# Rotary embedding of the attention queries and keys: half-turn by a permutation matmul, or by VectorE products that cross the partition halves

## The reference

```python
def _apply_rope(x, cos, sin):
    half = x.shape[-1] // 2
    x1, x2 = xf[..., :half], xf[..., half:]
    return jnp.concatenate([x1 * c - x2 * s, x2 * c + x1 * s], axis=-1)
...
def _dsa_branch(q, k, v, qi, ki, wi, rope_att, rope_idx, n_visible):
    q = _apply_rope(q.reshape(B_, T_, ATT_HEADS, ATT_HD), cos_a, sin_a)
    k = _apply_rope(k.reshape(B_, T_, ATT_KV_HEADS, ATT_HD), cos_a, sin_a)
    qi = _apply_rope(qi.reshape(B_, T_, IDX_HEADS, IDX_HD), cos_i, sin_i)
    ki = _apply_rope(ki.reshape(B_, T_, 1, IDX_HD), cos_i, sin_i)[:, :, 0]
    ...
        s = jnp.einsum('bqhd,bsd->bqhs', qib, ki)
        s = jnp.einsum('bqhs,bqh->bqs', jax.nn.relu(s), wib)
        _, idx = lax.top_k(s, topk)
        logits = jnp.einsum('bqgrd,bqkgd->bqgrk', qg, k_sel) * (ATT_HD ** -0.5)
        p = jax.nn.softmax(jnp.where(valid, logits, -jnp.inf), axis=-1)
        o = jnp.einsum('bqgrk,bqkgd->bqgrd', p, v_sel)
```

## Time and profile before

| what | us |
|---|---|
| time, median of 3 runs (lowest to highest) | 1267.67 (1267.56 to 1268.07) |
| profiled execution, first to last instruction | 1268.2 |
| TensorE busy in it | 1254.3 |
| VectorE busy | 919.6 |
| ScalarE busy | 699.2 |
| GpSimd busy | 154.3 |

### The profile page before, as it was taken

The page is one execution under the profiler, slowest core; times in us unless marked ns, Lnnn a source line. Parts: engine busy times, 40 slices in busy tenths (PEclk is TensorE's granted clock), DMA queues, the critical chain, the costliest instruction groups (busy, mean ns, idle before and its releaser), DMA issues.

```text
span 1268.2 us, 23324 instructions
## 1 busy us (share of the span) xinstructions
PE 1254.3 (99%) x9041; PEld 1169.6 (92%) x9041; DVE 919.6 (73%) x1290; ACT 699.2 (55%) x1082; POOL 154.3 (12%) x113
## 2 busy tenths in 40 slices
PE   9999999999999999999999999999999999999998
PEld 8997999999989998889998989999889998999986
DVE  6886874878778774447734547999758777999954
ACT  5556465654456343345354546666547567766642
POOL 0000142000000000000000001642200000464310
PEclk9999999999999999999999999999999999999999
DMA  7552332322355555555553444555564444454562
GB/s 300 189 173 101 133 134 101 133 68 68 152 197 188 195 179 185 198 170 182 183 209 109 156 173 167 198 169 195 194 221 171 162 154 163 167 188 175 197 224 93
DMA packets 30315, 212.83 MB, mean 168 GB/s; under 512 B 3488, under 2 KB 3616, under 8 KB 5152
## 3 DMA queue, kind: packets, MB, share of 16 engines
q1 hardware_dynamic: 29088, 206.53, 46.9%
q0 software_dynamic: 1152, 5.24, 1.1%
HBM read 210.71 MB, written 1.05 MB: 167 GB/s over the span
## 4 chain that ended last, share of the span: by engine, by line
PE 86%; DVE 8%; ACT 4%; DMA 1%; issue 1%; SPq 0%; DVEq 0%; ACTq 0%
PE lin L540 50%; PE lin L702 21%; DVE wlo L513 3%; PE lin L2883 2%; PE lin L567 2%; ACT whi L506 2%; PE lin L569 1%; DMA raw<-in_stream 1%; PE aux L2627 1%; PE aux L2599 1%; PE aux L2485 1%; ACT lm L1377 1%; PE aux L725 1%; PE aux L2745 1%; PE aux L2555 1%
## 5 line engine op out<-in xcount | busy, mean ns | idle before, releaser
L513 DVE TENSOR_TENSOR wlo<-raw,whi 128x2048 fp32r<-128x2048 f32 x183 | 427.4, 2338 | 170.8 <-ACT whi L506 170.1
L506 ACT CAST whi<-raw 128x2048 fp32r<-128x2048 f32 x192 | 365.3, 1906 | 179.5 <-DMA raw<-in_stream 147.0
L540 PE MATMUL lin<-xhi,whi 128*128 128x256 f32 (+2 forms) x1616 | 461.5, 286 | 1.0 <-DVE wlo L513 1.0
L540 PE MATMUL lin<-xlo,whi 128*128 128x256 f32 (+2 forms) x1616 | 457.0, 283 | 0.0
L540 PE MATMUL lin<-xhi,wlo 128*128 128x256 f32 (+2 forms) x1616 | 454.7, 281 | 0.0
L540 PEld LDWEIGHTS lin<-xhi,whi 128*128 128x128 f32 x1616 | 304.1, 188 | 3.0 <-DVE wlo L513 1.2
L540 PEld LDWEIGHTS lin<-xhi,wlo 128*128 128x128 f32 x1616 | 306.1, 189 | 0.0
L540 PEld LDWEIGHTS lin<-xlo,whi 128*128 128x128 f32 x1616 | 304.6, 189 | 0.4
L865 POOL TENSOR_TENSOR fu<-fs,ft 128x256 f32<-128x256 f32 x44 | 86.2, 1958 | 259.4 <-ACT fs L1479 259.4
L2292 DVE SCALAR_TENSOR_TENSOR ft<-fy,par,ft 128x254 f32<-128x254 f32 (+1 forms) x176 | 109.5, 661 | 5.9 <-DVE ft L2292 0.2
L540 PE MATMUL lin<-whi,xhi 128*128 128x256 f32 x256 | 74.2, 290 | 0.0
(11 more groups left out here) (454 smaller groups left out, 2123.2 us busy)
## 6 DMA issues: line engine op xcount, KB each, us to landing
raw<-in_stream SPq DMA_DIRECT2D x193, 1024.0 KB, 4.9
gp<-in_gains POOLq DMA_DIRECT2D x6, 512.0 KB, 3.9
c<-in_const SPq DMA_DIRECT2D x1, 1460.0 KB, 16.0
h<-in_x SPq DMA_DIRECT2D x2, 544.0 KB, 4.4
c<-in_const POOLq DMA_DIRECT2D x1, 1024.0 KB, 6.5
ht<-in_xtok POOLq DMA_DIRECT2D x1, 1024.0 KB, 9.6
out<-ht SPq DMA_DIRECT2D x1, 512.0 KB, 2.6
out<-ht SPq DMA_DIRECT2D x2, 256.0 KB, 2.0
```

Source lines behind the costliest of these rows:

```text
L506: nc.scalar.copy(whi[:, s0 % 4], raw[:, s0 % 4]).then_inc(hi_ready, 1)
L513: nc.vector.tensor_tensor(wlo[:, s0 % 4], raw[:, s0 % 4], whi[:, s0 % 4].bitcast(F32), ALU.subtract).then_inc(lo_ready, 1)
L540: ins = nc.tensor.matmul(out, a, b, start=start and n == 0, stop=stop and n == 2)
```

## The change

The rotations 3 to 8 lose their permutation matmul on TensorE. VectorE reads `x` itself: one product for each half, which reads one half of the partitions and writes the other (the sign is now in the sine table), then x times cosine into a second part of `ctmp`, then the sum. It is four instructions in place of three, and the first waits for ScalarE's copy of the projection, not for TensorE's matmul. The constant `turna` (128 columns) is gone. The index rotations 0 to 2 stay. The first five pieces of the first gate slot now follow one another.

```diff
@@ rotations on VectorE
                 n = x.shape[1]
+                if c == "cosa":
+                    rotate_halves(step)
+                    return
                 b = full(dve, name)
...
+            def rotate_halves(step):
+
+                name, x, W, c, sn, t0 = todo[step]
+                n = x.shape[1]
+                pair_done(dve, pair_first["ak"] if name[:6] == "rot_ak" else pair_first["aq"] + int(name[6:]))
+                turned = ctmp[:, 0, 0:n, 0:W]
+                for lo, hi in ((0, 64), (64, 0)):
+                    nc.vector.tensor_tensor(turned[lo:lo + 64], x[hi:hi + 64],
+                                            bc(cst(sn, lo=t0, n=W)[hi:hi + 64], n), ALU.mult)
+                straight = ctmp[:, 1, 0:n, 0:W]
+                own.link(nc.vector.tensor_tensor(straight, x, bc(cst(c, lo=t0, n=W), n), ALU.mult))
+                nc.vector.tensor_tensor(x, straight, turned, ALU.add).then_inc(S("rope"), 1)
                 dve.wait_ge(S("rope"), step + 1)
@@ order on TensorE
                 if step[0] == "rot":
-                    rotation(step[1])
+                    if step[1] < 3:
+                        rotation(step[1])
...
-            gate_part(0, 0, 2)
-            rotation(8)
-            gate_part(0, 2, 5)
+            gate_part(0, 0, 5)
             pe.wait_ge(S("rope"), 9)
@@ constants
+        if tag == "a":
+            c["sina"][dim // 2:] *= -1.0
+            continue
```

More of the change, by code:

```diff
@@ L71 @@
 CONST1 = [("ident", 128), ("window", 32), ("upper", 128), ("upper16", 128), ("ones16", 128), ("spread", 128), ("head", 8),
-          ("levels", 4 * 128), ("cosa", T1), ("sina", T1), ("cosi", T1), ("sini", T1), ("turna", 128),
+          ("levels", 4 * 128), ("cosa", T1), ("sina", T1), ("cosi", T1), ("sini", T1),
           ("turni", 128), ("past", 2 * T1)]
@@ L396, in program @@
         for step in PROJECT:
-            if step[0] == "rot":
+            if step[0] == "rot" and step[1] < 3:
                 use_next(ROT[step[1]])
@@ L404, in program @@
                 use_next({"l2": "l2sum"}.get(step[0], step[0]))
-        use_next(ROT[8])
         for t in range(2):
@@ L1659, in rotate @@
                 nc.vector.tensor_tensor(x, x, ctmp[:, 0, 0:n, 0:W], ALU.add).then_inc(S("rope"), 1)
+                dve.wait_ge(S("rope"), step + 1)
+            def rotate_halves(step):
[9 more added lines that the diff above has]
+                nc.vector.tensor_tensor(x, straight, turned, ALU.add).then_inc(S("rope"), 1)
                 dve.wait_ge(S("rope"), step + 1)
@@ L2379, in rotation @@
                 name, x, W, c, sn, t0 = todo[step]
[L2380 to L2388, removed]
+                pair_done(pe, 0 if name == "rot_ik" else pair_first["iq"] + int(name[6:]))
                 b = fill(name)
                 for n in range(x.shape[1]):
-                    ins = nc.tensor.matmul(b[:, n * W:n * W + W], turn, x[:, n], start=True, stop=True)
+                    ins = nc.tensor.matmul(b[:, n * W:n * W + W], cst("turni"), x[:, n], start=True, stop=True)
                 is_full(ins, name)
@@ L3023, in constants @@
             turn[m + dim // 2 if lo else m - dim // 2, m] = -1.0 if lo else 1.0
-        c["turn" + tag] = turn
+        c["turni"] = turn
     past = [np.where(pos[None, :] <= (META + t * P + i)[:, None], 0.0, -BIG) for t in range(2)]
```

## The result

The changed kernel takes 1271.79 us (median of 5 executions, 1271.19 to 1272.93) against 1267.67 (1267.56 to 1268.11) for the kernel before on the same chip: a ratio of 1.0032, 95% interval 1.0022 to 1.0043. It is slower, by 4.1 us. Its profiled execution has a span of 1271.1 us and a time of its own of 1272.93; in the executions whose span is told the time lies 1.7 to 1.9 us above the span (1.9 to 2.1 in those of e8).

What follows compares the result with a forecast made beforehand. VectorE's search and rotations were taken to bound the logits: 1.55 us of VectorE lateness plus 1.7 of clock fall gave +3.25, a median of 1270.9 us. The forecast's own range was 1270.0 to 1271.6, the outer one 1268.8 to 1272.6.

Steps and rivals of the forecast that it cites:

- The bound: Before the first logits, VectorE's second search and rotations set the time; from 146.89 to 164.69 us every step is VectorE's.
- The price of a half product: VectorE's rotations: half the partitions at full price, 0.73 us apart; a query pair takes 2.92 us at most, 2.68 at least.
- an overlap: Rival on VectorE's rotations: products overlap, +0.42 us, with a clock fall +2.1, 1269.8 us; chance 0.16.
- half a price for half the partitions: Rival on VectorE's rotations: a half product costs half of 0.69 us, so not slower; chance 0.05.
- VectorE's sum: VectorE up to rotation 8: 3.86 us added less 1.75 and 0.56 of idle time, +1.55 us.
- Both idle times: VectorE's idle 1.75 us before the index scores and 0.56 before rotation 5, both expected to be used up.
- The wait: TensorE before the first logits: arrives at about 159.92 us, logits start at 166.29, a wait of 6.4 us.
- The clock: TensorE behind the wait: one fall to half clock, 1.7 us lost; bounds nothing and 2.1 us.
- a clock that holds: Rival on TensorE's clock: it holds through the wait, so +1.55 us, 1269.2 us; chance 0.12.
- The sum: Whole kernel: 1.55 + 1.7 = +3.25 us, span 1268.2 to 1271.4, median 1267.67 to 1270.9 us.
- Nothing can fill it: TensorE's wait before the logits stays empty: the order is, with the remaining gate slots behind the wait.
- the removal counting in full: Rival: all 4.46 us of removed TensorE permutations are gained, 1263.2 us, needing VectorE done 4.5 us earlier; chance 0.03.

Runs made afterwards that it cites:

- e8: Kernel before, permutations kept, with seven more gate eighths ahead of the logits wait and GpSimd splitting weights without waiting for the last rotation: 1279.36 us.
- e2: Changed kernel with 26 unused matmuls of ones on TensorE in front of the wait for the ninth rotation: 1269.13 us.
- e3: Changed kernel with both half products reading and writing partitions 0 to 63, so nothing crosses and the half-turn is left out: 1270.36 us.
- e1: Kernel before, unchanged, run and profiled once more: 1268.03 us.
- e9: Changed kernel with 50 ready gate products ahead of the logits wait, ScalarE copying two gate tiles before the exponentials, GpSimd's order kept: 1269.10 us.
- e5: Changed kernel, no edit, run and profiled once more: 1271.62 us.
- e10: e9 with the softmax reordered, so ScalarE and VectorE copy turned probabilities earlier, in the middle of the softmax: 1264.23 us.
- e7: Changed kernel with seven more gate eighths ahead of the logits wait and GpSimd splitting weights without waiting for the last rotation: 1279.76 us.
- e4: Changed kernel with half products for rotations 3 to 5 only; rotations 6 to 8 use permutations again, first gate slot split: 1267.26 us.

## Why the prediction was right

**The bound.** Shown. VectorE's chain sets the logits in both kernels, and what it is late goes through to the end: 1.19 us at the logits and 1.26 in the time in e2, where the clock holds.

**The price of a half product.** Shown: 0.69 us for 64 partitions, none starting before its forerunner has ended. A rotation takes 2.86 us, the prediction's upper end being 2.92. The rivals of an overlap and of half a price for half the partitions are refuted by the rows of the profile after, and e3, with the start of rotation 5, shows that the crossing forbids the overlap.

**VectorE's sum.** +1.55 was forecast. The profile pair gives 166.09 - 164.74 = 1.35, e2 against e1 1.19, e9 against e1 1.55. Both idle times were used up as worked out; the sum is a little smaller, as a query pair's rotation grew by 0.68 and not by 0.74.

**The wait.** 6.2 us, forecast 6.4; TensorE came to it at 166.09 - 6.20 = 159.89, forecast 159.92, so the 4.46 us of permutations were read rightly.

**The clock.** One fall, 1.94 us, forecast 1.7; e2 shows that it was the wait that brought it. The rival of a clock that holds is refuted. That the size came out so near is in part luck: the 1.7 was half of a stretch behind narrow matmuls, and e3's fall, behind 5.1 us, costs 1.6 by the same reckoning (163.56 to 184.38, less 19.20).

**The sum.** +3.25 forecast, and a median of 1270.9; measured is 1271.79, inside the outer range (1268.8 to 1272.6) and 0.2 above the forecast's own (1270.0 to 1271.6). Its parts: 1.35 + 1.94 = 3.29 in the profile, 2.9 between the spans, 3.5 and 4.1 between the medians, 3.1 between the lower groups of e5. The terms hold; what the medians have above them goes with the fall at 122 us, which the prediction read in the earlier trace rows as a row of the kernel, and which is in some executions only. So the profiled execution of before was itself a long one of its kernel (its time would be 1268.2 + 1.8 = 1270.0, an estimate by the 1.8 us of the others), and "0.5 us above the median" compared a span with a time; that both profiles have this fall is why span less span came out right.

**What it had wrong.** "Nothing can fill it" is true of the order as written only; and of the removal counting in full it said that this needs VectorE 4.5 us earlier. e9 and e10 show otherwise: it needs other work for TensorE in the wait, and a softmax that does not become the next wait. With both, VectorE is as late as in the changed kernel and the time falls by 3.7 us. The prediction looked at one wait, and the one behind it, some 20 us later, had 0.4 us of slack at most (e1).

## What to carry to other kernels

Work taken off a full engine is a gain only if that engine has something else to do until the other one is done; look for the next work whose inputs are ready (here products with the high half of the weights), and then for the wait behind that one. A cheap-looking half instruction on VectorE costs a whole one, since the price goes by columns, and halves that cross partitions do not overlap. Before an instruction of GpSimd is moved, see which VectorE instructions with two SBUF inputs it will lie beside.

## What the runs showed of the hardware

GpSimd's subtraction of two SBUF tiles holds VectorE's instructions with two SBUF inputs that come up while it runs to its end (0.69 becomes 4.2 to 5 us), but not one with a PSUM input (0.69). A VectorE product that reads one half of the partitions and writes the other starts only when its forerunner has ended (0.70 apart, against 0.61). TensorE's clock fell after waits of 2.1 (e9), 5.1 (e3), 5.6 (e8), 6.2 and 10.9 us (e7) and not after one of 1.5 (e4), nor after e7's two of 1.5 and 1.2 us with 1.6 us of work between them. Behind the narrow matmuls at 122 us it falls in some executions of a program and not in others; their times differ by 1.2 to 1.7 us, if the two groups of times are those executions, as the profiled ones are and as the mean clocks of the groups suggest.
